# One sequence of heads through both attention mixers of a layer, in a four-layer fp32 transformer kernel

## Chip, cores and metric

The kernel runs on one core of a Trainium2 chip. The metric is the time of one execution on the device in microseconds, the median of several runs. Lower is better.

## What is computed

Two blocks of two layers run one behind the other over a sequence of 512 tokens of width 1024, in fp32. The first block's layers ("A") have three mixers side by side: sliding-window attention with sinks (swa, 6 heads), a pooling mixer, and latent attention with rotary keys (mla, 6 heads). The second block has a recurrent layer ("R") and a layer with forgetting attention (fox, 8 heads, "F"); both also attend to 256 memory tokens (xa, 4 heads). Cut to what matters here:

```
# layer A (twice)
proj  = rms_norm(x, attn_norm) @ w_in
out_a = swa_mixer(...)        # q, k normed per head; band of 128; softmax with a sink
out_b = pool_mixer(...)
out_c = mla_mixer(...)        # keys: a part per head, and one rotated part for all heads
x = x + concat([out_a, out_b, out_c]) @ w_out
x = x + (silu(h @ w_gate) * (h @ w_up)) @ w_down
# layer F (R has the recurrence in the place of fox)
y_mix, xq = fox_group(...)    # causal, decay per key
y_mem = memory_group(xq, mem) # full attention to the memory
x = x + concat([y_mix, y_mem]) @ w_out
x = x + square(relu(h @ w1)) @ w2
```

## The kernel before

Activations lie transposed (features on the partitions, 512 tokens along the row). Every fp32 product with a weight is three passes of TensorE over a high and a low part (`passes`, lines 853, 857 and 858). The weights come in chunks of 1 MB: SyncE loads a chunk into `raw`, GpSimd splits it into `wh` and `wl` (`split`, lines 647 and 652, about 7 us a chunk), TensorE uses it. Each engine has its own program and its own in-order queue, written out by hand; semaphores join them. `Banks` counts the uses of each of the eight PSUM banks.

A mixer is a `Mixer` with its heads, and units of one or two heads. For a unit, `prep` makes the normed queries and keys: TensorE spreads the row scales to banks 6 and 7 (line 1122), VectorE multiplies into `t` (lines 1744, 1752), ScalarE copies the high parts to `qh` and `key` (line 1374), GpSimd subtracts for the low parts (`ql`, `key`, line 697) and gives `qk_ready`, for which VectorE's next `prep` waits. A head then goes like this:

- TensorE, `score_rows` in two halves (banks 0, 1; lines 1158 and 1161 for causal, 1169 and 1171 for the band, 1174 for full): scores by query, for the row maxima;
- VectorE, `maxima` in two halves (lines 2138 to 2152) into `mx`, part of tile `sm`;
- ScalarE, `diagonals` in two halves: the maxima as diagonal blocks `dg`;
- TensorE, `score_columns` (banks 2, 3; lines 1200 to 1209): scores by key, minus the maxima. A causal head has four blocks and uses each of the two banks twice;
- ScalarE, `exponentials` into `pt`; swa adds the sink's exponential, `es`;
- TensorE, `weighted` (bank 4; lines 1226, 1235, 1236, 1241): values times `pt`;
- ScalarE, `reciprocal` (`rt`, logarithm and exponential), VectorE, `out` (`sq`), GpSimd, `mixed`: into `act`. For swa the denominator is first added by VectorE (`es<-ps,es`, in `out`), and `reciprocal` waits for it (`den_ready`); for the others it reads a bank.

The orders within step `hd` of the loop over heads are: TensorE rows of `hd+1` (first half), `prep`, columns of `hd`, rows of `hd+1` (second half), `weighted(hd-1)`; VectorE first maxima of `hd+1`, `prep`, `out(hd-2)`, second maxima; ScalarE `reciprocal(hd-2)`, first diagonals of `hd+1`, `exponentials(hd)`, `prep`, second diagonals; GpSimd `prep`, a weight chunk in two of the heads, `mixed(hd-2)`.

`attention` is called once for each mixer. At the end of the first mixer's loop, in step `hd == m.heads`, `start(nxt)` begins the next: for mla the rotated part of the keys (ts, then a copy and a subtraction into each of the two key tiles) and unit 0. Unit 1 and the first rows follow at the head of the next call:

```
prep(m, 1)
score_rows(0, 0)
score_rows(0, 1)
for hd in range(m.heads + 1):
```

Of the kernel before, what the change touches and what calls it, by code (L numbers as in the profile page):

```python
# [28 lines left out]
P = 128  # L29
# [169 lines left out]
class Mixer:  # L199


    def __init__(self, kind, name, heads, per_unit, rows, scale, tile0, place, kidx):
# [7 lines left out]
    def slot(self, u):  # L210
        return u % 2
# [10 lines left out]
    def half(self, h):  # L222

        return h % 2 if self.per_unit == 2 else 0

# [37 lines left out]
MLA = Mixer("causal", "mla", 6, 1, 96, MLA_SCALE, 5, 1, 6)  # L263
FOX = Mixer("causal", "fox", 8, 2, 64, 1.0, 0, 0, 4)
XA = Mixer("full", "xa", 4, 1, 128, XA_SCALE, 4, 1, 0)


def build(nc, a):
    with ExitStack() as ctx:
# [65 lines left out]
        key_pairs = {"swa": [[key[0], key[1]]], "mla": [[key[0]], [key[1]]], "xa": [[key[0]], [key[1]]],  # L335
# [21 lines left out]
        dgs = {"swa": (dg0, dg1_swa), "mla": (dg0, dg1), "fox": (dg0, dg1), "xa": (dg0, dg1)}  # L357
# [263 lines left out]
        def _(pool):  # L621
# [7 lines left out]
            def split(s, nblk, first=False, slot_done=None, early=False):  # L629
# [4 lines left out]
                if slot_done is not None:  # L634
                    pool.wait_ge(ready[slot_done], bk.filled(slot_done, -1))
# [116 lines left out]
            def summed(hd):  # L752


                if hd >= 2:
                    pool.wait_ge(ready[5], bk.filled(5, hd - 2))
                for b in (2, 3):
                    pool.wait_ge(free[b], bk.emptied(b, hd))
# [3 lines left out]
            def attention(m, nxt=None, chunk_at=None, recurrence=False, second_at=None, slot_done=None):  # L762
                prep(m, 1)
                for hd in range(m.heads + 2):
                    if m.starts(hd):
                        prep(m, m.starts(hd))
                    if m.name == "xa":
                        if hd >= 2:
                            mixed(m.vrow(hd - 2), m.tile(hd - 2))
                        if hd < m.heads:  # L770
                            summed(hd)
                    if hd == chunk_at:

                        split_all(1, BLOCKS)
                    if hd == second_at:

                        split_all(1, BLOCKS, slot_done)
                    if m.name == "mla" and hd == m.heads:
# [3 lines left out]
                    if hd >= 2 and m.name != "xa":  # L782
                        mixed(m.vrow(hd - 2), m.tile(hd - 2))
                    if hd == m.heads and nxt:
                        prep(nxt, 0)
                    if recurrence and hd < 4:
                        mixed(slice(0, P), hd)
                bk.close(m.uses())

            s = 0  # L790
            for l, kind in enumerate(layers):
# [3 lines left out]
                if kind == "A":  # L795
# [3 lines left out]
                    attention(SWA, MLA, 3)  # L799
                    attention(MLA, second_at=3, slot_done=7)  # L800
                elif kind == "R":
                    bk.close(USES_IN_R)
                    prep(XA, 0)
                    attention(XA, None, 2, True, second_at=4, slot_done=3)
# [24 lines left out]
        def _(pe):  # L829
# [295 lines left out]
            def prep(m, u):  # L1125
                spread_to(6, u, u, m.place)
# [3 lines left out]
                elif m.name == "mla":  # L1130
                    spread_to(7, 1 + u, 6 + u // 2, m.place)
                elif m.name == "fox":
                    spread_to(7, u, 4 + u, m.place)
                else:
                    spread_to(7, u, u, 1, M_MEM, slice(64, P))

            def start(m):

                pe.wait_ge(rs_ready, rsr.up(2 if m.name == "xa" else 1))
                if m.name == "mla":  # L1140
                    spread_to(7, 0, 9, m.place)
                prep(m, 0)

            def attention(m, vcols, keys, heads=None, nxt=None, s_pool=None):
# [3 lines left out]
                def score_rows(hd, half):  # L1148
# [1317 lines left out]
```

## Time and profile before

| | |
|---|---|
| median of 3 runs | 2461.61 us (2461.43 to 2462.5) |
| the profiled execution | 2467.87 us, span of its trace 2466.1 us |
| TensorE | busy 2329.9 us (94%), mean granted clock 0.974 |
| GpSimd | busy 1669.3 us (68%) |
| VectorE | busy 1030.9 us (42%) |
| ScalarE | busy 502.2 us (20%) |
| DMA | 84 GB/s over the span |

The profile gives each instruction with its engine, its line and what it waited for. PE is TensorE, DVE is VectorE, ACT is ScalarE and POOL is GpSimd; PEclk is the clock that TensorE was granted, as a share of 2.4 GHz. An idle time in square brackets stands ahead of the instruction on its own engine, with what ended it. Most instructions of the vector engines have the line of a helper, so tiles tell more than lines: `t<-qc` is mla's `prep`, `key<-ts` the rotated part, `es<-ps,es` swa's denominator, `sq<-ps,rt` the product in `out`.

### The profile page before, as it was taken

The page shows a single profiled execution, that of the slowest core. Times are in us where ns is not written, and L with a number is a line of the kernel's source. Part 1 is how long each engine was busy: PE and PEld are TensorE (multiplying, and loading weights), DVE is VectorE, ACT ScalarE, POOL GpSimd, SP SyncE. Part 2 cuts the span into 40 slices and gives each one's busy share as a digit, 9 for nine tenths or more (in the row PEclk, how much of TensorE's full clock was granted, in tenths as well). Part 3 has the DMA queues.
Part 4 walks back from the last instruction along what each step waited for, and adds up shares of the span by engine and source line. Part 5 has one row for each costly group of instructions (what it writes and reads, how often), then busy time and mean ns, then how long its engine had stood idle before and what let it go on. Part 6 is the DMA issues. An engine that isn't in the chain of part 4 may idle for free.

```text
span 2466.1 us, 29684 instructions
## 1 busy us (share of the span) xinstructions
PE 2329.9 (94%) x11024; PEld 1900.3 (77%) x11024; DVE 1030.9 (42%) x1304; ACT 502.2 (20%) x955; POOL 1669.3 (68%) x1378
## 2 busy tenths in 40 slices
PE   6978999999997899999998799999999798999999
PEld 4767788888776678888887478888888676888887
DVE  6663533322366353332237645215334334540430
ACT  3244211110134421111012511001111263100000
POOL 5565677777756567777777677767766566776774
PEclk9988999999998899999999899999999999999999
DMA  4300222223330022222332123222232200222222
GB/s 146 116 18 18 77 94 102 87 85 98 113 108 18 18 79 92 102 92 81 103 116 103 35 85 102 89 98 102 87 118 86 86 35 18 87 101 102 87 101 85
DMA packets 37892, 207.93 MB, mean 84 GB/s; under 512 B 3580, under 2 KB 10364, under 8 KB 16936
## 3 DMA queue, kind: packets, MB, share of 16 engines
q1 hardware_dynamic: 37800, 206.70, 23.9%
q8 instruction: 58, 0.95, 0.2%
q14 instruction: 34, 0.28, 0.0%
HBM read 204.55 MB, written 2.13 MB: 84 GB/s over the span
## 4 chain that ended last, share of the span: by engine, by line
PE 60%; POOL 3%; DVE 2%; ACT 2%; issue 2%; DMA 0%; DVEq 0%; POOLq 0%; ACTq 0%; SPq 0%
PE ps L853 18%; PE ps L857 18%; PE ps L858 18%; POOL wl L652 1%; PE ps L1226 1%; PE ps L1200 1%; ACT rt L1374 1%; PE ps L1241 0%; DMA raw<-w_in_f 0%; POOL wh L647 0%; PE ps L1204 0%; PE ps L1201 0%; PE ps L1202 0%; POOL act L737 0%; DVE sq L1744 0%
## 5 line engine op out<-in xcount | busy, mean ns | idle before, releaser
L652 POOL TENSOR_TENSOR wl<-raw,wh 128x512 fp32r<-128x512 f32 (+1 forms) x776 | 1030.5, 1360 | 0.2
L647 POOL TENSOR_SCALAR wh<-raw 128x1024 fp32r<-128x1024 f32 (+1 forms) x388 | 427.8, 1122 | 586.9 <-PE ps L853 458.5
L853 PE MATMUL ps<-h,wh 128*128 128x512 f32 x1576 | 619.2, 393 | 27.1 <-DVE h L1752 20.2
L858 PE MATMUL ps<-h,wl 128*128 128x512 f32 x1576 | 615.2, 390 | 0.0
L857 PE MATMUL ps<-h,wh 128*128 128x512 f32 x1576 | 615.0, 390 | 0.0
L853 PE MATMUL ps<-act,wh 128*128 128x512 f32 x1120 | 437.4, 391 | 1.0 <-DVE x L1744 1.0
L857 PE MATMUL ps<-act,wh 128*128 128x512 f32 x1120 | 436.0, 389 | 0.0
L858 PE MATMUL ps<-act,wl 128*128 128x512 f32 x1120 | 435.9, 389 | 0.0
L853 PEld LDWEIGHTS ps<-h,wh 128*128 128x128 f32 x1576 | 296.8, 188 | 95.9 <-issue 24.7
L857 PEld LDWEIGHTS ps<-h,wh 128*128 128x128 f32 x1576 | 297.1, 189 | 61.8 <-issue 1.0
L858 PEld LDWEIGHTS ps<-h,wl 128*128 128x128 f32 x1576 | 296.8, 188 | 62.0
L1744 DVE TENSOR_TENSOR x<-x,ps 128x512 f32<-128x512 f32 x80 | 55.0, 688 | 482.7 <-PE ps L858 482.1
L853 PEld LDWEIGHTS ps<-act,wh 128*128 128x128 f32 x1120 | 210.5, 188 | 46.9 <-issue 3.1
L857 PEld LDWEIGHTS ps<-act,wh 128*128 128x128 f32 x1120 | 210.4, 188 | 44.0 <-issue 0.5
L858 PEld LDWEIGHTS ps<-act,wl 128*128 128x128 f32 x1120 | 210.4, 188 | 43.7
L1374 ACT ACTIVATE h<-x,vec 128x512 fp32r<-128x512 f32 x64 | 46.3, 724 | 438.3 <-DVE x L1744 430.9
L1374 ACT ACTIVATE act<-t 128x512 f32 (+1 forms) x64 | 40.5, 633 | 461.4 <-DVE t L1752 461.4
L697 POOL TENSOR_TENSOR ql<-t,qh 128x512 fp32r<-128x512 f32 x30 | 38.9, 1296 | 132.5 <-ACT key L1374 94.3
L1744 DVE TENSOR_TENSOR t<-ps,rstd 128x512 f32<-128x512 f32 x108 | 74.7, 692 | 107.7 <-PE ps L858 106.4
L1744 DVE TENSOR_TENSOR ssq<-ssq,sq 128x512 f32<-128x512 f32 (+1 forms) x80 | 80.7, 1008 | 85.6 <-ACT sq L1374 84.8
L1744 DVE TENSOR_TENSOR nt<-ps,rstd 128x512 f32<-128x512 f32 x44 | 30.4, 692 | 194.1 <-PE ps L858 194.0
L1744 DVE TENSOR_TENSOR act<-t,act 128x512 f32 (+1 forms) x64 | 67.7, 1058 | 64.1 <-ACT act L1374 64.1
(324 smaller groups left out, 2672.2 us busy)
## 6 DMA issues: line engine op xcount, KB each, us to landing
raw<-w_gu SPq DMA_DIRECT2D x44, 1024.0 KB, 4.8
raw<-w_up SPq DMA_DIRECT2D x32, 1024.0 KB, 4.8
raw<-w_down_b SPq DMA_DIRECT2D x32, 1024.0 KB, 4.8
raw<-w_down_a SPq DMA_DIRECT2D x32, 704.0 KB, 4.0
raw<-w_in_a SPq DMA_DIRECT2D x14, 1024.0 KB, 4.9
raw<-w_in_f SPq DMA_DIRECT2D x13, 1024.0 KB, 4.9
raw<-w_in_r SPq DMA_DIRECT2D x11, 1024.0 KB, 4.9
raw<-w_out_a SPq DMA_DIRECT2D x8, 1024.0 KB, 8.1
```

Of the source, the lines that this page charges most:

```text
L647: pool.tensor_scalar(hi_s[:, part], raw[s][:, part], 1.0, 1.0, ALU.mult, ALU.mult).then_inc(hi_done, 1)
L652: return pool.tensor_tensor(lo_s[:, part], raw[s][:, part], hi_s[:, part].bitcast(F32), ALU.subtract)
L697: pool.tensor_tensor(out, in0, in1, op).then_inc(hi_done, 1)
L853: first = pe.matmul(out, w_hi, v_hi, start=start, stop=False)
L857: pe.matmul(out, w_hi, v_lo, start=False, stop=False)
L858: return pe.matmul(out, w_lo, v_hi, start=False, stop=stop)
L1200: pe.matmul(out, k_hi[:, kc], qh[s][:, qc_], start=True, stop=False)
L1226: last = pe.matmul(ps[4][:, j * P:T], vcols(hd, j), pt[:, j * T:j * T + n], start=j == 0, stop=j == keys - 1)
L1374: return sc.activation(out, in_, f, **kw)
L1744: dve.tensor_tensor(out, in0, in1, op).then_inc(sig.sem, 1)
```

## The change

`attention` takes a sequence of mixers, (swa, mla) or (fox, xa), and runs one loop over all their heads, numbered `g`. Its last two steps belong to the sequence and no longer to each mixer. `begins` says at which step a unit is prepared: units 0 and 1 of the later mixer in the last two steps of the earlier one. The first rows of the later mixer are scored in the step ahead of its first head, as for any head. The rotated part of mla's keys has its own function, `rotation`, in step `g == 3`. For these overlaps mla gets key tiles of its own, `key_mla`, a second `dg` tile of its own, and the other of the two query slots; `use` adds the earlier mixer's uses of a bank to the count. GpSimd's chunks stand at steps 3 and 9 for (swa, mla), and at 4 and 7 for (fox, xa); in each loop a `prep` stands ahead of the chunk. The layer with xa alone makes one call as before. The diff, cut to its core:

```diff
+        self.earlier = after.uses() if after else {}
+    def use(self, b, u):
+        return self.earlier.get(b, 0) + u
     def slot(self, u):
-        return u % 2
+        return (u + (self.name == "mla")) % 2
...
+XA_F = Mixer("full", "xa", 4, 1, 128, XA_SCALE, 4, 1, 0, FOX)
+ROTATE_AT = 3
+def begins(seq):
+    at, first = {}, 0
+    for i, m in enumerate(seq):
+        if i:
+            at[first - 2], at[first - 1] = (m, 0), (m, 1)
+        for hd in range(m.heads):
+            if m.starts(hd):
+                at[first + hd] = (m, m.starts(hd))
+        first += m.heads
+    return at
...
+        key_mla = [view(f"key_mla{s}", A_AT + 32768 + 29696 + s * 4096, [2, T], F32R) for s in range(2)]
+        dg1_mla = view("dg1_mla", A_AT + 32768 + 45056, [TB, P], F32R)
...
# GpSimd
+            def attention(seq, chunks_at, recurrence=False):
+                prep(seq[0], 1)
+                for g in range(n + 2):
+                    if g in at:
+                        prep(*at[g])
+                    cross = g < n and order[g][0].name == "xa"
+                    if cross:
+                        if g >= 2:
+                            finished(g)
+                        summed(*order[g])
+                    if g in chunks_at:
+                        split_all(1, BLOCKS, chunks_at[g])
...
+                    if g >= 2 and not cross:
+                        finished(g)
...
-                    attention(SWA, MLA, 3)
-                    attention(MLA, second_at=3, slot_done=7)
+                    attention((SWA, MLA), {3: None, 9: (7, 2)})
...
-                    attention(FOX, XA, 4, second_at=7, slot_done=0)
-                    attention(XA)
+                    attention((FOX, XA_F), {4: None, 7: (0, -1)})
...
# TensorE
+                prep(seq[0], 1)
+                score_rows(*order[0], 0)
+                score_rows(*order[0], 1)
+                for g in range(n + 1):
+                    if g + 1 < n:
+                        score_rows(*order[g + 1], 0)
+                    if g in at:
+                        m, u = at[g]
+                        if u == 0 and m.name == "xa":
+                            start(m)
+                        else:
+                            prep(m, u)
+                    if seq[-1].name == "mla" and g == ROTATE_AT:
+                        rotation()
+                    if g < n:
+                        score_columns(*order[g])
...
+                    if g + 1 < n:
+                        score_rows(*order[g + 1], 1)
+                    if g:
+                        weighted(*order[g - 1])
...
# ScalarE
+                for g in range(n + 2):
+                    if g >= 2:
+                        reciprocal(*order[g - 2])
+                    if g + 1 < n:
+                        diagonals(*order[g + 1], 0)
+                    if g < n:
+                        exponentials(*order[g])
+                    if g in at:
+                        prep(*at[g], order[g])
+                    if g + 1 < n:
+                        diagonals(*order[g + 1], 1)
...
# VectorE
+            def rotation():
+                b, u = 7, MLA.use(7, 0)
+                dve.wait_ge(ready[b], bk.filled(b, u))
+                r = slice(64, P)
+                tt(ts[r, :], krp[r, :], ps[b][r, :], ALU.mult, bk.empties(b, u))
+                for both in key_mla:
+                    split(ts[r, :], both[r, 0, :], both[r, 1, :], chain)
...
+                for g in range(n + 2):
+                    if g + 1 < n:
+                        maxima(*order[g + 1], 0)
+                    if g in at:
+                        m, u = at[g]
+                        prep(m, l, u)
+                    if seq[-1].name == "mla" and g == ROTATE_AT:
+                        rotation()
...
+                    if g >= 2:
+                        out(*order[g - 2])
+                    if g + 1 < n:
+                        maxima(*order[g + 1], 1)
```

## Rows read from the trace of the kernel before

**Rows 1.** The page's part 4: the chain by line, shares of the span.

```profile
PE ps L853 18%; PE ps L857 18%; PE ps L858 18%; POOL wl L652 1%; PE ps L1226 1%; PE ps L1200 1%; ACT rt L1374 1%; PE ps L1241 0%; DMA raw<-w_in_f 0%; POOL wh L647 0%; PE ps L1204 0%; PE ps L1201 0%; PE ps L1202 0%; POOL act L737 0%; DVE sq L1744 0%
```

**Rows 2.** Windows, layer 2: us, busy of PE, PEld, DVE, ACT, POOL; PEclk, DMA, GB/s.

```profile
765.00:788.00 23.00, 20.87 (x166) 19.56 (x165) 12.22 (x21) 15.37 (x32) 14.57 (x14) 1.00 0.14 47
788.00:806.00 18.00, 11.42 (x34) 7.93 (x35) 11.92 (x19) 6.91 (x14) 9.07 (x8) 0.58 0.00 0
806.00:846.00 40.00, 37.57 (x194) 30.44 (x192) 16.68 (x30) 25.39 (x58) 21.55 (x19) 0.94 0.04 11
```

**Rows 3.** Timeline, TensorE, layer 2, swa to mla: start, us, engine, line; idle before.

```profile
791.62 0.79 PE L1122 MATMUL ps<-rs,spread 64*128 64x512 f32 x1 [3.07 <-DVE ts L1744]
...
803.29 0.47 PE L1158 MATMUL ps<-key,qh 128*128 128x128 f32 x1 [1.65 <-ACT key L1374]
...
805.48 0.79 PE L1200 MATMUL ps<-qh,key 128*128 128x512 f32 x1
```

**Rows 4.** Timeline, layer 2, head 4 of swa: TensorE, VectorE, ScalarE.

```profile
776.03 0.38 PE L1200 MATMUL ps<-qh,key 128*128 128x256 f32 x1 [0.18 <-ACT dg L1374]
...
777.23 0.69 DVE L1744 TENSOR_TENSOR es<-ps,es 64x512 f32<-64x512 f32 x1
...
777.96 0.63 ACT L1374 ACTIVATE rt<-es 64x512 f32<-64x512 f32 x1 [1.98 <-DVE es L1744]
...
779.34 0.68 DVE L1744 TENSOR_TENSOR sq<-ps,rt 64x512 f32<-64x512 f32 x1 [1.42 <-issue]
...
782.26 0.69 ACT L1374 ACTIVATE dg_swa<-ident,sm 128x128 fp32r<-128x128 f32 x2 [0.86 <-DVE sm L2152]
...
783.01 0.39 PE L1200 MATMUL ps<-qh,key 128*128 128x256 f32 x1 [1.10 <-ACT dg_swa L1374]
```

**Rows 5.** Timeline, TensorE, layer 2: first column product of mla's heads 1 and 2.

```profile
813.95 0.50 PE L1200 MATMUL ps<-qh,key 128*128 128x512 f32 x1
...
821.19 0.50 PE L1200 MATMUL ps<-qh,key 128*128 128x512 f32 x1
```

**Rows 6.** VectorE in head 3; copy and subtraction of key and of cqn; GpSimd's split.

```profile
770.28 0.24 DVE L2152 TENSOR_SCALAR sm<-sm,vec 128x2 f32<-128x2 f32 x1
...
773.87 0.69 DVE L2147 TENSOR_REDUCE sm<-ps 128x2 f32<-128x512 f32 x1 [0.67 <-PE ps L1171]
...
L1748 DVE TENSOR_SCALAR key<-ts x4: 424/424/425, 174.6 to 793.7; 64x512 fp32r<-64x512 f32 x4
L1744 DVE TENSOR_TENSOR key<-ts,key x4: 689/1164/1643, 175.1 to 794.2; 64x512 fp32r<-64x512 f32 x4
...
L1748 DVE TENSOR_SCALAR cqn<-t x4: 1398/1402/1411, 69.4 to 692.9; 128x512 fp32r<-128x512 f32 x4
L1744 DVE TENSOR_TENSOR cqn<-t,cqn x4: 693/1179/1667, 70.8 to 694.4; 128x512 fp32r<-128x512 f32 x4
...
771.47 5.00 POOL L652 TENSOR_TENSOR wl<-raw,wh 128x512 fp32r<-128x512 f32 x4
```

**Rows 7.** Timeline, VectorE, mla's head 1: the next unit waits for GpSimd.

```profile
815.51 0.69 DVE L1744 TENSOR_TENSOR t<-qc,ps 128x512 f32<-128x512 f32 x1 [1.69 <-POOLq L750]
```

**Rows 8.** Windows, layer 2: behind two idle stretches; the granted clock is PEclk.

```profile
744.80:750.00 5.20, 5.19 (x25) 5.20 (x26) 3.42 (x12) 1.18 (x3) 4.68 (x6) 0.52 0.00 0
...
852.40:856.00 3.60, 3.60 (x7) 1.91 (x8) 0.00 (x0) 0.00 (x0) 3.06 (x3) 0.56 0.02 5
```

**Rows 9.** Timeline, last layer, fox to xa: GpSimd's split and first sum; TensorE.

```profile
2024.70 5.00 POOL L652 TENSOR_TENSOR wl<-raw,wh 128x512 fp32r<-128x512 f32 x4
...
2033.19 2.42 PE L1226 MATMUL ps<-pt_f,vof 128*128 128x512 f32 x8 [1.70 <-DVE sq L1744]
...
2040.94 0.80 PE L1174 MATMUL ps<-key,qh 128*128 128x256 f32 x2 [4.21 <-ACT key L1374]
...
2050.04 1.28 POOL L760 TENSOR_TENSOR ts<-pt 128x512 f32<-128x512 f32 x1 [0.24 <-POOL key L697]
...
2065.55 1.98 PE L1241 MATMUL ps<-pt0b,fxv 128*128 128x512 f32 x4 [2.14 <-DVE sq L1744]
```

More of the change, by code:

```diff
@@ L750, in prep, with summed @@
                 pool.sem_inc(qk_ready, 1)
-            def summed(hd):
+            def summed(m, hd):
                 if hd >= 2:
-                    pool.wait_ge(ready[5], bk.filled(5, hd - 2))
+                    pool.wait_ge(ready[5], bk.filled(5, m.use(5, hd - 2)))
                 for b in (2, 3):
-                    pool.wait_ge(free[b], bk.emptied(b, hd))
+                    pool.wait_ge(free[b], bk.emptied(b, m.use(b, hd)))
                 pt = pts["xa"][hd % 2]
                 pool.tensor_tensor(pt_sum[hd % 2], pt[:, 0:T], pt[:, T:2 * T], ALU.add).then_inc(sum_ready, 1)
[L762 to L778, printed above, removed]
@@ new lines, in attention, with finished @@
+            def attention(seq, chunks_at, recurrence=False):
+                order, at = heads_of(seq), begins(seq)
+                n = len(order)
+                def finished(g):
+                    m, hd = order[g - 2]
+                    mixed(m.vrow(hd), m.tile(hd))
+                prep(seq[0], 1)
[9 more added lines that the diff above has]
+                        split_all(1, BLOCKS, chunks_at[g])
+                    if g == n and seq[-1].name == "mla":
@@ L790, in _ @@
+                    if recurrence and g < 4:
+                        mixed(slice(0, P), g)
+                for m in seq:
+                    bk.close(m.uses())
             s = 0
@@ L1238, in weighted @@
                     else:
-                        for j in range(keys):
-                            pe.wait_ge(free[2 + j], bk.emptied(2 + j, hd))
+                        for j in range(m.key_blocks()):
+                            pe.wait_ge(free[2 + j], bk.emptied(2 + j, m.use(2 + j, hd)))
                             last = pe.matmul(ps[4][:, :], vcols(hd, j), pt[:, j * T:(j + 1) * T],
@@ L2121, in start, with rotation, attention, maxima @@
                     halves(key_pairs[m.name][0])
-                if m.name == "mla":
-                    dve.wait_ge(ready[7], bk.filled(7, 0))
-                    r = slice(64, P)
-                    tt(ts[r, :], krp[r, :], ps[7][r, :], ALU.mult, bk.empties(7, 0))
-                    for s in range(2):
-                        split(ts[r, :], key[s][r, 0, :], key[s][r, 1, :], chain)
-                prep(m, l, 0)
-            def attention(m, l, nxt=None):
-                def maxima(hd, half):
+                prep(m, l, 0)
+            def rotation():
+                b, u = 7, MLA.use(7, 0)
[4 more added lines that the diff above has]
+                    split(ts[r, :], both[r, 0, :], both[r, 1, :], chain)
+            def attention(seq, l):
+                def maxima(m, hd, half):
                     mxs = mx[hd % 2]
```

240 lines of the change are left out of this document (101 added, 139 removed).

## The prediction

> **What bounds the kernel now.** I read the page first: TensorE is busy 94% of the span, and the chain that ended last runs through TensorE, more than half the span in the three lines of the weight products, which the change leaves alone [rows 1]. So a gain or a loss can only come from stretches in which TensorE waits. Next I cut the three attention stages with a change of mixer into windows. In the second layer TensorE works 20.9 of 23 us while the six heads of swa run at full clock, 11.4 of 18 us across the change to mla at a granted clock of 0.58, and 37.6 of 40 us among the heads of mla [rows 2]. The first layer has the second's idle times to 0.01 us, plus one more of 1.36. Then the timeline gave the waits behind the hole: 3.07 us ended by VectorE (the rotated key part) and 1.65 us ended by ScalarE (key), with two smaller ones between them 6.6 in all [rows 3], 7.9 in the first layer. In the last layer, from fox to xa, it is 1.70 and 4.21 us [rows 9]. These are what the change can take away; the reader should see that they are a drained pipeline, and that it drains for 22.5 us between the score columns of swa's last head (783.01) and those of mla's first (805.48) [rows 3, 4].
>
> **Costs of nothing.** `use()`, `heads_of` and `begins` are worked out as the program is built. The new views `key_mla` and `dg1_mla` and mla's other slot issue nothing. The layer with one mixer keeps its order. SyncE's queue isn't touched. What is left is order, so I follow the start of each head's score columns, numbered c0, c1 and so on through the joined sequence, in the second layer. Before: c4 at 776.03, c5 783.01, c6 (mla's first head) 805.48, c7 813.95, c8 821.19 [rows 3 to 5]. From c8 on the order is the old one.
>
> **How I check the arithmetic.** In head 4 as it is, `out(2)` starts es at c4+1.20, ScalarE's logarithm follows at +1.93, VectorE's product at +3.31 to +3.99, the diagonal at +6.23, and c5 comes at +6.98 [rows 4]. One point matters for all that follows: VectorE runs `out` ahead of `maxima(.., 1)`, ScalarE runs `reciprocal` ahead of `diagonals(.., 0)` and `exponentials`, and both queues are in order. For swa the reciprocal waits for es of VectorE. So what is put ahead of `out` in VectorE's queue delays the reciprocal, the exponentials and the next diagonals.
>
> **Step 1, the rotation in head 3.** It takes 0.69 us for ts, and twice a copy and a subtraction. In the hole these took 0.42 and 0.69 to 1.64, but in head 3 GpSimd splits a weight chunk until 776.5 [rows 6]. The nearest rows of the same pair beside a split are cqn's, 1.40 and a median of 1.18 [rows 6]. Lower bound 0.69+2(0.42+0.69)+0.2 = 3.1, upper 0.69+2(1.40+1.67) = 6.8 with the longest cqn subtraction; I take the cqn medians, since the split runs throughout, 0.69+2(1.40+1.18)+0.15 = 6.0. VectorE comes free at 770.52 [rows 6], so es starts at 776.55, the product ends 2.8 us later at 779.3, the diagonal starts 2.24 us behind that (both distances from [rows 4]) and takes 0.7, so c4 = 782.3, **+6.3** (lower bound +3.3). TensorE idles 773.8 to 779.4, since `weighted(2)` waits for bank 4. The stall of 3.07 us is moved, not hidden: all that covers it in head 3 is the 0.67 us for which VectorE waits ahead of the maxima [rows 6]. Trainium skill, "SBUF — State Buffer", section "Who interferes with whom": an SBUF to SBUF tensor_scalar in a two-port mode and a GpSimd instruction exclude each other. It would give the 1.40; by the clean 0.42 and 0.69 the head would be 2.9 us shorter. By that rule the cqn row, with its 1.40 beside a split, agrees.
>
> **Step 2, head 4 takes mla's first unit.** VectorE does 0.69+0.74 us ahead of es, ScalarE 1.15 between exponentials and the last diagonals. es at +2.05, product to +4.85, reciprocals to +4.1, exponentials and es to +6.4, copies (`qh`, `key`) to +7.55, diagonal to +8.25. TensorE has the first rows of mla and two spreads more, 1.1 us, and waits for `key`: c5 = c4+8.8 = 791.1; before 6.98, so **+1.8**.
>
> **Step 3, head 5, second unit.** VectorE's `prep` waits for GpSimd's ql and key remainder: 1.27+1.27 us after `key`, as VectorE's t waits for GpSimd today [rows 7]; so, from c5, t starts at +1.6, es +3.1, product to +5.9, exponentials and es to +7.45, copies to +8.6. c6 = c5+9.8 = 800.9. Before 22.47: **-12.7**. Here is the whole gain.
>
> **Step 4, heads 6 and 7 (mla 0 and 1).** Here a new wait appears. Causal columns use banks 2 and 3 twice, so block 2 waits for the exponential of block 0. That stands in ScalarE's queue behind the reciprocal of swa's head 4, behind VectorE's es, behind `prep`, behind GpSimd. Counted from c6: GpSimd 1.5, prep 3.05, es 3.8, reciprocal 5.15, diagonal 5.85, exponential 6.45; TensorE stood since 2.1, **4.4 us idle**. Then columns to 7.6, rows 8.35, `weighted` 10.1 (1.8 us that used to run in the hole), rows and spreads: c7 = c6+11.25 = 812.15 (before 8.47, +2.8). Head 7 likewise, with es at +2.05, block 2 at 5.45 (3.3 us idle) and mla's own `weighted` 2.4: c8 = c7+10.85 = 823.0 (before 7.24, +3.6). From head 8 on the reciprocals are mla's, which wait for TensorE alone.
>
> Sum at the clock as it is: +6.3+1.8-12.7+2.8+3.6 = **+1.8 us** a layer; with the clean rotation -1.2.
>
> **Step 5, the clock.** Behind the idle 741.3 to 744.8, the stretch 744.8 to 750.0 ran at 0.52, which is the lower of the two levels, 1.2 GHz; behind 848.7 to 852.4, 3.6 us at 0.56 [rows 8]. That costs 5.2 x 0.48 = 2.5 and 3.6 x 0.44 = 1.6 us of TensorE's work. Before has such a stretch after its own hole, and it is in its c values. After has three idles of over 3 us (5.6, 4.4, 3.3), each ahead of work that is on the chain: 3 x 2.2 = **+6.5 us** a layer. Bounds: 0, and about 15 if the clock stays down from 778 to 822, as it did for 20 us from 791 on.
>
> **Step 6, fox to xa.** c6 and c7 of fox slip by 0.4 and 1.4 (two spreads and xa's rows), xa's first columns come at 2033.6 instead of 2042.38. But in head 7 GpSimd now does xa's `prep` 1 first, which waits for ScalarE until 2031.8, and only then the split of 7.1 us that ended at 2029.7 [rows 9]. So `prep` (2.0 us) to 2033.9, split to 2041.1, `mixed` (1.9) to 2043.0, `prep` 2 to 2045.1, `mixed` to 2047.0, the first sum (1.28) to 2048.3; before it ended at 2051.3 [rows 9]. VectorE's prep of unit 3 waits for 2045.1 with `out(7)` behind it, so xa's first `weighted` comes at 2047.1, TensorE idle for 5.6 us. The tail then runs in today's rhythm of one head per 5 us, its last `weighted` at 2061.8 instead of 2065.55 [rows 9]: **-3.8 us**, of 8.8.
>
> **Total.** 2 x (1.8+6.5) - 3.8 = +12.8 us. The profiled execution took 2467.87 us (span 2466.1), so 2480.7 by its clock; the median of the three runs is 6.3 lower, 2461.61, so **2474**.
>
> **Rivals.** (a) *The clock falls no more than before* (for: the second layer holds 1.00 from 765 to 788 through idles of 1.1 us; against: all six idles over 3 us in these stages are followed by the lower level): 2 x 1.8-3.8 = 0, **2462**. With the clean rotation 2456. (b) *The clock stays down over the joint*: 2 x (1.8+15)-3.8, **2491**. (c) *The join works as it reads*, faster: rotation, prep and reciprocals lie in VectorE's and ScalarE's spare time (VectorE is busy 12.2 of 23 us), and the holes go, 6.6+7.9+5.9 = 20.4, with some of the low clock: **2440**. It holds if block 2 of mla's columns doesn't wait; against it stands the order of the two queues. (d) *It isn't overlapped at all*, mla's first rows waiting for swa's end: against it, `key` of mla's first unit is due at 789.9, before c5; then the hole stays and head 4's 1.8 us is added: **2465**.
>
> **Chances.** Forecast 0.43, (a) 0.24, (b) 0.10, (c) 0.19, (d) 0.04. A measurement of this kernel tells 0.2%, 4.9 us, from no change. (a) is split over no change and faster, (c) is faster: faster 0.25, same 0.22, slower 0.53. The range leaves out most of (c) and the edge of (b): 2451 to 2491; the forecast's own range is 2467 to 2484.
>
> **What would show it.** Right: a wait of about 5 us of TensorE in head 3 that ends with a diagonal or bank 4, es of `out(1)` some 6 us behind the maxima, copies of the rotation near 1.4; in mla's first two heads the third block of columns waiting on pt for 4.4 and 3.3 us; a granted clock of about 0.5 behind each; in the last layer the GpSimd split at about 2034 and `weighted` of xa waiting for it; swa's last to mla's first columns near 10 us. Wrong: if c4 comes less than 4 us later, if c4 to c8 takes clearly less than 41 us, or the clock reads 1.00 across them.

## The result: 0.8% slower

The changed kernel takes 2485.09 us (median of 4 runs, 2480.67 to 2486.93), the kernel before beside it 2462.06 (2461.43 to 2464.39): a ratio of 1.0076, 95% interval 1.0063 to 1.009. The forecast was 2474, slower, in a range of 2451 to 2491. The profiled execution took 2486.93 us, its span is 2485.2 against 2466.1.

The page of the kernel after, its parts 1 (busy time of each engine) and 4 (the chain that ended last, by line), beside the table of before and [rows 1]:

```profile
PE 2338.3 (94%) x11024; PEld 1908.4 (77%) x11024; DVE 1030.7 (41%) x1304; ACT 499.7 (20%) x955; POOL 1670.7 (67%) x1378
...
PE ps L886 18%; PE ps L890 18%; PE ps L891 18%; POOL wl L684 2%; PE ps L1264 1%; POOL wh L679 1%; PE ps L1236 1%; POOL act L769 1%; DMA raw<-w_in_f 0%; ACT rt L1416 0%; PE ps L1279 0%; DVE t L1795 0%; PE ps L1240 0%; PE ps L1237 0%; PE ps L1238 0%
```

The busy times of VectorE, ScalarE and GpSimd move by under 3 us. GpSimd's split (`wh`, `wl`) has come into the chain with 3%, where it had 1%. So the question is again where TensorE stands. For that I laid the same VectorE instruction at the end of each stage of the two traces side by side and took the differences of the two starts. These are worked out from the rows, not rows themselves:

| stage | after later than before, at its end | added in it | forecast |
|---|---|---|---|
| first layer (swa, mla), with the stage behind it | +3.5 us | +3.5 | +8.3 |
| second layer, likewise | +10.8 | +7.3 | +8.3 |
| third layer (xa alone, with the recurrence) | +18.0 | +7.2 | 0 |
| last layer (fox, xa) | +19.1 | +1.1 | -3.8 |

Each line is one execution of each kernel, and it scatters. The kernels of experiments 1 and 8 have the same code in the first two layers as the kernel after, and add 3.3 and 5.6 us, and 6.2 and 5.9 us there. The kernel of experiment 2 has the code of before in them, and adds -2.4 and -0.1 us. So a line of the table is good to 2 or 3 us.

**Layer 2.** Timeline of TensorE after the change: the first column product of head 3 (c3) and so on to c8, and the waits between them; answers to [rows 3 to 5]. mla's heads begin with c6; the line of c6 or c7 is followed by that of their block 2, the third of their four blocks of columns.

```profile
773.63 0.39 PE L1236 MATMUL ps<-qh,key 128*128 128x256 f32 x1
...
783.03 0.80 PE L1274 MATMUL ps<-pt,vos 128*128 128x128 f32 x2 [5.60 <-DVE sq L1787]
...
787.36 0.39 PE L1236 MATMUL ps<-qh,key 128*128 128x256 f32 x1
...
796.05 0.38 PE L1236 MATMUL ps<-qh,key 128*128 128x256 f32 x1
...
802.21 0.49 PE L1274 MATMUL ps<-pt,vos 128*128 128x128 f32 x2 [2.26 <-DVE sq L1787]
...
806.93 0.79 PE L1236 MATMUL ps<-qh,key_mla 128*128 128x512 f32 x1
...
812.40 0.38 PE L1236 MATMUL ps<-qh,key_mla 128*128 128x256 f32 x1 [2.02 <-ACT pt L1416]
...
818.61 0.50 PE L1236 MATMUL ps<-qh,key_mla 128*128 128x512 f32 x1
...
823.51 0.48 PE L1236 MATMUL ps<-qh,key_mla 128*128 128x256 f32 x1 [2.83 <-ACT pt_a L1416]
...
831.98 0.50 PE L1236 MATMUL ps<-qh,key_mla 128*128 128x512 f32 x1
```

The join does what it says: from the last head of swa to the first of mla (c5 to c6) there are 10.9 us where there were 22.5. What it takes comes back around it: c3 to c4 takes 13.7 us (before 6.0, c3 stood at 770.03), c6 to c7 11.7 (8.5), c7 to c8 13.4 (7.2). c3 to c8 is 58.35 us against 51.16.

What head 3 waits for stands in VectorE's queue. Timeline of VectorE after, head 3; and GpSimd's split of the same time. Answers to [rows 6].

```profile
773.89 0.23 DVE L2199 TENSOR_SCALAR sm<-sm,vec 128x2 f32<-128x2 f32 x1
774.15 0.69 DVE L1787 TENSOR_TENSOR ts<-krp,ps 64x512 f32<-64x512 f32 x1
774.88 0.51 DVE L1791 TENSOR_SCALAR key_mla<-ts 64x512 fp32r<-64x512 f32 x1
775.42 1.65 DVE L1787 TENSOR_TENSOR key_mla<-ts,key_mla 64x512 fp32r<-64x512 f32 x1
777.11 1.38 DVE L1791 TENSOR_SCALAR key_mla<-ts 64x512 fp32r<-64x512 f32 x1
778.53 1.63 DVE L1787 TENSOR_TENSOR key_mla<-ts,key_mla 64x512 fp32r<-64x512 f32 x1
780.20 0.68 DVE L1787 TENSOR_TENSOR es<-ps,es 64x512 f32<-64x512 f32 x1
...
775.08 6.21 POOL L684 TENSOR_TENSOR wl<-raw,wh 128x512 fp32r<-128x512 f32 x4
```

Between the maxima and `es` of `out(1)` lie 6.05 us of rotation, and behind `es` the reciprocal, the product and `weighted(2)`, as in [rows 4].

The clock, windows after in layer 2 (us, busy of PE, PEld, DVE, ACT, POOL; PEclk, DMA, GB/s); answers to [rows 2, 8]:

```profile
779.20:786.00 6.80, 2.96 (x14) 2.97 (x15) 3.26 (x5) 4.07 (x9) 4.02 (x4) 0.51 0.44 154
...
803.10:809.90 6.80, 6.80 (x23) 5.35 (x22) 3.13 (x6) 2.17 (x5) 4.44 (x4) 0.50 0.00 0
...
823.60:830.40 6.80, 6.80 (x20) 4.97 (x21) 1.25 (x2) 2.63 (x7) 2.83 (x3) 0.50 0.01 2
```

With one of 3.4 us from 813.3 on (PEclk 0.52) these are four spells at the lower level (1.2 GHz), 23.8 us in sum. The first begins within the idle time of 5.60 us, the others start behind those of 2.26, 2.02 and 2.83; before there is one of 20.5 us (790.6 to 811.1, PEclk 0.50).

**Third layer.** This was not foreseen. Timeline of GpSimd, first before, then after: the split of the second chunk (`wh`, `wl`) and the first operation of the mixes of cross heads 2 and 3 (`act<-sq`).

```profile
1424.98 0.62 POOL L701 TENSOR_SCALAR act<-sq 128x512 fp32r<-128x512 f32 x1
...
1427.17 2.07 POOL L647 TENSOR_SCALAR wh<-raw 128x1024 fp32r<-128x1024 f32 x2 [0.22 <-POOL act L737]
1429.20 5.02 POOL L652 TENSOR_TENSOR wl<-raw,wh 128x512 fp32r<-128x512 f32 x4
1434.31 0.62 POOL L701 TENSOR_SCALAR act<-sq 128x512 fp32r<-128x512 f32 x1
```

```profile
1438.14 2.06 POOL L679 TENSOR_SCALAR wh<-raw 128x1024 fp32r<-128x1024 f32 x2 [0.22 <-POOL act L769]
1440.16 5.02 POOL L684 TENSOR_TENSOR wl<-raw,wh 128x512 fp32r<-128x512 f32 x4
1445.27 0.62 POOL L733 TENSOR_SCALAR act<-sq 128x512 fp32r<-128x512 f32 x1
```

`cross = g < n and ...` is false at g = 4, where the second chunk stands. So `finished(4)`, the mix of cross head 2, moved from ahead of the split to behind it, and now two mixes wait behind 7.1 us of splitting: the one at 1445.27 and, from 1447.32 on, that of head 3. TensorE's output projection waits for the first of them, 1.90 us until 1447.29, and runs at a granted clock of 0.83 for the 10.1 us behind it.

### The profile page after: what moved, and what is told of

Same layout as the page of the kernel before. It is cut to its first block, busy times and chain, and to the rows that moved or that the text cites. A ratio compares the mean times of both kernels' runs of the same rounds, so it can differ in the third digit from the quotient of the medians.

```text
span 2485.2 us, 29688 instructions
## 1 busy us (share of the span) xinstructions
PE 2338.3 (94%) x11024; PEld 1908.4 (77%) x11024; DVE 1030.7 (41%) x1304; ACT 499.7 (20%) x955; POOL 1670.7 (67%) x1378
## 3 DMA queue, kind: packets, MB, share of 16 engines
q1 hardware_dynamic: 37800, 206.70, 23.8%
## 4 chain that ended last, share of the span: by engine, by line
PE 59%; POOL 4%; DVE 2%; issue 2%; ACT 2%; DMA 0%; DVEq 0%; POOLq 0%; ACTq 0%; SPq 0%
PE ps L886 18%; PE ps L890 18%; PE ps L891 18%; POOL wl L684 2%; PE ps L1264 1%; POOL wh L679 1%; PE ps L1236 1%; POOL act L769 1%; DMA raw<-w_in_f 0%; ACT rt L1416 0%; PE ps L1279 0%; DVE t L1795 0%; PE ps L1240 0%; PE ps L1237 0%; PE ps L1238 0%
## 5 line engine op out<-in xcount | busy, mean ns | idle before, releaser
L886 PE MATMUL ps<-h,wh 128*128 128x512 f32 x1576 | 619.9, 393 | 26.0 <-DVE h L1795 19.1
```

Source lines behind the costliest of these rows:

```text
L886: first = pe.matmul(out, w_hi, v_hi, start=start, stop=False)
```

## The experiments

Times are medians; a ratio is to the kernel before on the same chip, with its 95% interval. Its median lay between 2462.06 and 2468.01 us from one set of runs to another, so kernels are compared by their ratios. "Stage" is the difference to before at the end of each stage, as in the table above, from the one profiled execution.

**1. The one-mixer layer's order as before.** In GpSimd's `attention`, in the kernel after:

```diff
-                    cross = g < n and order[g][0].name == "xa"
+                    cross = order[min(g, n - 1)][0].name == "xa"
                     if cross:
                         if g >= 2:
                             finished(g)
-                        summed(*order[g])
+                        if g < n:
+                            summed(*order[g])
```

> The changed kernel with one edit: in the layer with xa alone GpSimd does mixed of head 2 ahead of the weight chunk again, as before the change. Theory (the order of GpSimd's queue in that layer costs, 5.0 us from the last mixed to the first x): TensorE's out projection no longer waits 1.9 us for mixed of head 2, the layer gives back about 5 us, 2480 us. Rival (what that layer lost is only the phase of the clock): no change, 2485.

2478.75 us, ratio 1.005 (1.0033 to 1.0067). By the ratios that is 6.4 us less than after. The stage of the third layer adds -0.05 us instead of +7.2.

**2. The same order put into the kernel before, alone.** There the mix of cross head 2 goes behind the chunk; that of head 3 stood behind it already (1434.31 in the rows before):

```diff
+                    late = recurrence and hd >= m.heads
                     if m.name == "xa":
-                        if hd >= 2:
+                        if hd >= 2 and not late:
                             mixed(m.vrow(hd - 2), m.tile(hd - 2))
...
-                    if hd >= 2 and m.name != "xa":
+                    if hd >= 2 and (m.name != "xa" or late):
```

> The kernel before, with one part of the change alone: in the layer with one mixer (four cross heads) GpSimd splits the second chunk of weights ahead of mixed(2) and mixed(3), as the kernel after does. Theory: that order costs by itself what this layer lost, the queue of 5.0 us of subtractions in front of the last two mixes, so the layer's stage grows by 4 to 5 us and the time by the same, near 2467 (ratio 1.0018). Rival: the layer was longer only because its columns fell into other clock periods; then this kernel is at 2462, ratio 1.000, and the last mix follows the split with nobody waiting for it.

2472.99 us, ratio 1.0028 (1.0015 to 1.004), which is 6.9 us (3.7 to 9.9). The stage of that layer adds 5.0 us. Timeline of TensorE, the first product of the output projection that waits for the mix, and the window behind it (granted clock 0.79):

```profile
1431.87 0.50 PE L854 MATMUL ps<-act,wh 128*128 128x512 f32 x1 [3.31 <-POOL act L737]
```

```profile
1431.87:1440.00 8.13, 8.13 (x29) 6.51 (x30) 0.00 (x0) 0.00 (x0) 1.91 (x2) 0.79 0.26 109
```

So one moved mix costs about 5 us by itself: 3.3 us of waiting, and 1.7 behind it, where the products run at the lower clock. In the kernel after, 3.8 of the 7.2 us come at the place of the mix and 3.3 ahead of it, where the granted clock was 0.91 against 0.94 before. The kernel of experiment 12, whose order in this layer is repaired, has 3.2 us there too, also at 0.91. So I read these 3.3 us as scatter of the clock from execution to execution, but no run isolates them. In kernels that kept the moved order the stage added 4.0 to 7.2 us.

**3. The rotation in two pieces**, behind the second maxima of steps 3 and 4:

```diff
-                    if seq[-1].name == "mla" and g == ROTATE_AT:
-                        rotation()
...
                     if g + 1 < n:
                         maxima(*order[g + 1], 1)
+                    if seq[-1].name == "mla" and g in (ROTATE_AT, ROTATE_AT + 1):
+                        rotation(g - ROTATE_AT)
```

(`rotation(0)` makes ts and the first split, `rotation(1)` the second split.)

> The changed kernel with the rotation in two pieces, each behind the second maxima: ts and the first key tile at the end of step 3, the second key tile at the end of step 4. Theory (the rotation ahead of out(1) holds the den, the reciprocal and bank 4): columns 3 to 4 fall from 13.7 us to about 6.5, columns 4 to 5 rise by 1 to 1.5, the first piece is partly beside the split; 5 to 6 us a layer, 2474 us. Rival (head 3 is held by something else, the split or the exponentials): c3 to c4 stays over 11 us, 2485.

2475.57 us, ratio 1.0037 (1.0025 to 1.005). Timeline of VectorE, the five instructions of the rotation, then TensorE's c3, c4, c5 with a wait between:

```profile
773.79 0.69 DVE L1787 TENSOR_TENSOR ts<-krp,ps 64x512 f32<-64x512 f32 x1
774.52 0.74 DVE L1791 TENSOR_SCALAR key_mla<-ts 64x512 fp32r<-64x512 f32 x1
775.29 0.99 DVE L1787 TENSOR_TENSOR key_mla<-ts,key_mla 64x512 fp32r<-64x512 f32 x1
...
782.96 0.42 DVE L1791 TENSOR_SCALAR key_mla<-ts 64x512 fp32r<-64x512 f32 x1
783.42 0.69 DVE L1787 TENSOR_TENSOR key_mla<-ts,key_mla 64x512 fp32r<-64x512 f32 x1
```

```profile
768.53 0.38 PE L1236 MATMUL ps<-qh,key 128*128 128x256 f32 x1
...
774.97 0.38 PE L1236 MATMUL ps<-qh,key 128*128 128x256 f32 x1
...
781.88 0.80 PE L1274 MATMUL ps<-pt_a,vos 128*128 128x128 f32 x2 [3.13 <-DVE sq L1787]
...
787.07 0.58 PE L1236 MATMUL ps<-qh,key 128*128 128x256 f32 x1
...
802.06 0.58 PE L1236 MATMUL ps<-qh,key_mla 128*128 128x256 f32 x1 [4.38 <-ACT pt L1416]
```

c3 to c4 is back at 6.4 us, c4 to c5 went from 8.7 to 12.1. The five instructions take 3.5 us in sum, not the 5.9 of the kernel after: GpSimd's split ends at 774.98, within the first copy, and GpSimd is idle beside the second piece. c3 to c8 is 52.7 us, 5.6 less than after.

**4. The whole rotation, uncut, behind the second maxima of step 3**, which tells place from cut:

```diff
-                    if seq[-1].name == "mla" and g == ROTATE_AT:
-                        rotation()
...
                     if g + 1 < n:
                         maxima(*order[g + 1], 1)
+                    if seq[-1].name == "mla" and g == ROTATE_AT:
+                        rotation()
```

> The kernel after, with the whole rotation still in step 3 but behind the second maxima instead of ahead of swa's output. It tells the rotation's place from its being cut in two. With two pieces behind the second maxima, c3 to c4 was 6.44 us and c4 to c5 12.1 (18.5 together, after: 22.4), and VectorE's five instructions took 0.69, 0.74, 0.99, 0.42 and 0.69 us, 3.5 together, where in the kernel after, beside GpSimd's split of weights, they took 6.0. Theory: place does it: the rotation stands behind GpSimd's split, is short, and holds up no output of step 3; c3 to c5 is again 18 to 19 and the time near the run with two pieces, 2476. Rival: the cut does it: the second split, now in a row with the first, holds up the maxima of step 4 and the two outputs behind them, c3 to c5 is 20 to 22 us, and the time 2480 or more.

2479.55 us, ratio 1.005 (1.0034 to 1.0067). c3 to c4 6.4 us, c4 to c5 14.1, together 20.6: both theories have a part. In the profiles the place gives 1.9 us (22.4 to 20.6) and the cut another 2.0 (to 18.5); in the first layer it is 2.8 and 1.4 (22.7, 20.0, 18.5). The intervals of the two times overlap, so the time alone doesn't tell the cut from the uncut rotation. The rotation's own instructions take 4.5 us here, 5.9 after and 3.5 in two pieces. The cut keeps the second split from the front of step 4, where it holds up two maxima, mla's `prep` and `out(2)` behind them.

**5. Products that nobody reads in the idle times** of the kernel after (20 in head 3, 12 and 10 ahead of block 2 in mla's first two heads):

```diff
+                    if seq[-1].name == "mla" and g == 3:
+                        pe.wait_ge(free[7], bk.emptied(7, MLA.use(7, 0)))
+                        for _ in range(20):
+                            pe.matmul(ps[7][:, :], neg_ones_r[:, :], qh[SWA.slot(1)][:, :], start=True, stop=True)
                     if g:
                         weighted(*order[g - 1])
...
+                        if m.name == "mla" and j == 2 and hd < 2:
+                            pe.wait_ge(free[5], bk.emptied(5, SWA_HEADS - 1))
+                            for _ in range((12, 10)[hd]):
+                                pe.matmul(ps[5][:, :], neg_ones_r[:, :], qh[s][:, :], start=True, stop=True)
```

> The changed kernel with products that nobody reads in TensorE's three long idle times of a layer: 20 of 128x512 ahead of weighted(2) in step 3, 12 and 10 ahead of block 2 of the columns of mla's heads 0 and 1. Nothing is waited for less. Theory (part of the loss is TensorE at the lower clock behind its idle times, 5.4 us of the 58.3 from columns 3 to 8): the clock reads 1.00 there and a layer gains about 4 us, 2477 us. Rival (the chain is all latency of the other engines, the clock costs nothing): the same time or up to 3 us more, 2485 to 2488.

2478.69 us, ratio 1.0044 (1.0027 to 1.006). Window of layer 2, from c3 to the idle time of head 7:

```profile
771.99:820.00 48.01, 39.03 (x243) 33.01 (x243) 26.08 (x42) 21.26 (x48) 21.18 (x19) 1.00 0.06 23
```

The granted clock is 1.00 up to 820; one spell at the lower level follows (0.62 in 821.6 to 825). The five distances from c3 to c8 are 12.61, 8.70, 9.93, 11.05 and 13.24 us, 55.5 in sum, against 58.35 after, and 56.6 and 56.9 in the kernels of experiments 1 and 8 with the same code. By the ratios the time is 7.9 us less, 3.9 a layer.

**6. The same in the kernel before**: 13, 6 and 7 unread products in the three idle times of TensorE in the change of mixer.

```diff
                 elif m.name == "mla":
+                    if u == 0:
+                        pe.wait_ge(free[5], bk.emptied(5, SWA.heads - 1))
+                        unread(13)
                     spread_to(7, 1 + u, 6 + u // 2, m.place)
...
+                        if m.name == "mla" and (hd, i) == (0, 2):
+                            unread(6)
...
+                    if m.name == "mla" and hd == 1 and half == 0:
+                        unread(7)
```

> The kernel before, with 13, 6 and 7 products of 512 columns, whose result nobody reads, in the three idle times of TensorE between the mixers (3.07, 1.41 and 1.65 us in layer 2). Nothing in the order or the waits of the other work is changed. It prices the clock by itself: before, the granted clock is at its lower level from 790.6 to 811.1, and the first mla columns stand in it. Theory: that low clock follows from the idle times and costs 4 to 7 us a layer (the busy time of 793 to 811, about 13 us, at half speed, less what waits for other engines anyway), so 2450 to 2456, ratio 0.996, and the stretch from c5 to c6 falls from 22.5 to about 19. Rival: the clock falls from what was done before the idle times or the columns are held up by other engines, and nothing is gained: 2462 or, with the products in the way, 2464.

2463.25 us, ratio 0.9982 (0.9972 to 0.9992): a real gain, but small. Windows of the same stretch of layer 2, before and with the products:

```profile
790.60:811.10 20.50, 15.97 (x52) 12.54 (x52) 12.16 (x20) 7.12 (x15) 9.07 (x8) 0.50 0.00 1
```

```profile
790.00:811.00 21.00, 17.45 (x88) 13.88 (x87) 13.01 (x23) 11.37 (x26) 9.56 (x8) 0.92 0.01 2
```

The clock is mostly held up, and the gain is smaller than the 4 to 7 us a layer of the theory: the ratio gives 4.4 us for both layers, 2.2 each. The profiles say 3.1 and 3.4, but before's profiled execution was 6 us above its median, and the unchanged first layer of experiment 2 is already 2.4 us shorter than its own. In layer 2, c5 to c6 falls by only 0.9 us and c6 to c7 by 2.4; in layer 1, c5 to c6 doesn't fall at all (22.77 against 22.47). So of the 22.5 us hole at most one microsecond is TensorE's clock.

**7. VectorE's outputs of swa ahead of mla's preparation** (steps 4 to 7):

```diff
                     if g + 1 < n:
                         maxima(*order[g + 1], 0)
+                    first = g >= 4 and order[g - 2][0].name == "swa"
+                    if first:
+                        out(*order[g - 2])
                     if g in at:
                         m, u = at[g]
                         prep(m, l, u)
...
-                    if g >= 2:
+                    if g >= 2 and not first:
                         out(*order[g - 2])
```

> The changed kernel with VectorE doing out of swa's heads 2 to 5 ahead of prep of mla's units instead of behind it (steps 4 to 7). Theory (es behind prep holds the reciprocal, and with it the exponentials and block 2): columns 4 to 8 fall from 44.6 us to about 33, the idle ahead of block 2 from 2.0 and 2.8 us to under 1.7; 11 us a layer, 2463 us. Rival (block 2 waits for its own columns and exponential, not for the queue): 4 to 8 stays over 42 us, 2485.

2458.44 us, ratio 0.9971 (0.996 to 0.9981): faster than before, with the rotation still in head 3 and the third layer's moved mix still in. Timeline of TensorE, c3, c4, c6 and c8 with two waits (c5 and c7 stand at 783.14 and 797.59):

```profile
761.43 0.39 PE L1236 MATMUL ps<-qh,key 128*128 128x256 f32 x1
...
770.83 0.80 PE L1274 MATMUL ps<-pt,vos 128*128 128x128 f32 x2 [5.61 <-DVE sq L1787]
...
775.78 0.38 PE L1236 MATMUL ps<-qh,key 128*128 128x256 f32 x1
...
789.95 0.50 PE L1236 MATMUL ps<-qh,key_mla 128*128 128x512 f32 x1
...
792.99 0.38 PE L1236 MATMUL ps<-qh,key_mla 128*128 128x256 f32 x1 [0.98 <-ACT pt L1416]
...
805.91 0.50 PE L1236 MATMUL ps<-qh,key_mla 128*128 128x512 f32 x1
```

The rotation's wait stays (5.61). From c4 on the distances are 7.4, 6.8, 7.6 and 8.3 us, 30.1 in sum, where the kernel after has 44.6 and before has 45.2. The waits for block 2 fall to 0.98 and 1.07 us, those ahead of `weighted` in heads 4 and 5 are gone, and from 777 to c8 the granted clock is 1.00. The 14.5 us that c4 to c8 is shorter are the delays of steps 2 to 4 and the spells of low clock that came with them; the time is 5 us below what was expected.

**8. The outputs of fox ahead of xa's preparation**, likewise (`g >= 6` in the last layer alone).

> The kernel after, with the last two outputs of fox (steps 8 and 9, and those of steps 6 and 7) ahead of the cross mixer's preparation on VectorE. In the kernel after, TensorE idles 5.83 us before the cross mixer's first weighted sums (2060.94 to 2066.77) until VectorE's output of fox head 7, which stands behind a preparation that waited 5.53 us for GpSimd. Theory: VectorE's place in line is what is waited for, the idle time falls to about 1 us, and 3 to 5 us of it reach the end, 2481 (ratio to before 1.006). Rival: GpSimd's split (2053.1 to 2060.2) is the bound through the cross mixer's own units, and the idle time comes back one head later: no change, 2485.

2484.51 us, ratio 1.0075 (1.0063 to 1.0087): no change that can be measured. The idle time of 5.83 us has become one of 3.25 and, behind the first `weighted`, one of 1.47 until GpSimd's sum for xa. Timeline of TensorE at the last join, and of VectorE's output of fox head 7:

```profile
2062.88 3.43 PE L1279 MATMUL ps<-pt,fxv 128*128 128x512 f32 x4 [3.25 <-DVE sq L1787]
```

```profile
2062.13 0.69 DVE L1787 TENSOR_TENSOR sq<-ps,rt 64x512 f32<-64x512 f32 x1 [4.48 <-POOL act L769]
```

The output now waits for GpSimd's mix, which is queued behind the split. So GpSimd's split holds this join, wherever VectorE's output stands.

**9. Four repairs together**: experiments 1, 3, 7 and 8 in one kernel.

> The kernel after with four repairs together: GpSimd's order in the one-mixer layer as before, the rotation's two splits in two steps (3 and 4) behind the second maxima, VectorE's outputs of swa ahead of mla's preparation (steps 4 to 7), and those of fox ahead of the cross mixer's. If the repairs add up, from the run with the outputs ahead (2458.4): -4.9 for the one-mixer layer, -5 in each attention layer for the rotation (there 14.35 us from c3 to c4, 6.44 with the rotation in two, less what its second piece costs in the next step), -3 at the last join: 2441, ratio 0.991. Rival: the second piece pushes the preparation of mla's second unit in step 5, whose lateness was hidden so far, and half of the rotation's gain goes: 2447.

2443.01 us, ratio 0.991 (0.9895 to 0.9924). Window of layer 2 from c3 to c8, before, after, and here:

```profile
770.03:821.19 51.16, 42.28 (x230) 35.29 (x230) 27.47 (x46) 26.77 (x57) 26.07 (x24) 0.80 0.06 21
```

```profile
773.63:831.98 58.35, 43.81 (x230) 37.01 (x230) 28.07 (x47) 25.51 (x57) 27.25 (x24) 0.80 0.05 19
```

```profile
758.04:798.68 40.64, 34.44 (x229) 29.36 (x229) 27.66 (x46) 25.79 (x57) 23.04 (x21) 1.00 0.08 27
```

The same 229 or 230 products; 40.6 us instead of 51.2 or 58.4, at a granted clock of 1.00 throughout. VectorE does 27.5 to 28.1 us of work in each of the three: what changed is its order.

**10. The same, with the rotation's pieces in steps 2 and 3** (`ROTATE_AT = 2`).

> As the run with all four repairs, but the rotation's two pieces in steps 2 and 3, ahead of any of mla's preparations. Theory: in step 3 a piece behind the second maxima moved nothing (c3 to c4 6.44 us), in step 4 one did (c4 to c5 12.1 us); a piece in step 2 meets swa's last preparation (unit 2) and costs under 2 us, so this is 2 to 4 us a layer better than with steps 3 and 4: 2436. Rival: step 2 is as full as step 4 and nothing is gained, 2441 to 2445.

2448.58 us, ratio 0.9932 (0.9921 to 0.9944). No better, by the medians rather worse: c3 to c8 is 42.7 us, with 2.3 us of idle ahead of `weighted` in head 3 and a granted clock of 0.88. Nothing is gained, as the rival had it, though its time was 2441 to 2445.

**11. and 12. GpSimd's second chunk of the last layer in step 6 or 5 instead of 7**, on top of the four repairs (`{4: None, 6: (0, -1)}`, `{4: None, 5: (0, -1)}`).

> The kernel with all four repairs, and GpSimd's split of the second chunk in the last layer one step earlier (step 6, behind the cross mixer's first preparation, instead of step 7). With only VectorE's outputs moved ahead the idle time at the last join stayed at 3.25 and 1.47 us, the first until fox head 7's output, which waited 4.48 us for GpSimd's mix, queued behind the split (2052.9 to 2060.0). Theory: GpSimd's split in step 7 is the bound; in step 6 it fills 3.1 us in which GpSimd was idle, and 2 to 4 us go: 2440, ratio 0.990. Rival: it only moves the wait to the cross mixer's second preparation, within 1 us of the kernel with four repairs (2443).

> The same with the split in step 5, where GpSimd was idle 3.7 us before the cross mixer's first preparation. Theory: it ends near 2045, 2 us after that preparation could have begun, and hides more than in step 6: 2 to 5 us less than with four repairs, 2439. Rival: with the first chunk's split just one step earlier (2028 to 2035), outputs of fox wait for the mixes behind it, and as much comes back: 2443.

2441.51 us, ratio 0.9883 (0.9867 to 0.9899), and 2441.98, ratio 0.9886 (0.9871 to 0.99). Timeline of TensorE at the last join with the chunk in step 5: fox's last `weighted`, xa's first, and the largest wait left.

```profile
2017.71 2.39 PE L1265 MATMUL ps<-pt_f,vof 128*128 128x512 f32 x8
...
2023.23 1.88 PE L1280 MATMUL ps<-pt,fxv 128*128 128x512 f32 x4
...
2039.79 1.98 PE L1280 MATMUL ps<-pt0b,fxv 128*128 128x512 f32 x4 [2.14 <-DVE sq L1788]
```

The stage of the last layer adds -0.4 us with the four repairs, -3.0 with the chunk in step 6 and -9.7 in step 5, the 5.83 us idle time gone. The times don't show this difference: the two medians lie within 0.5 us, and both intervals overlap that of experiment 9. In the profile of the step 5 kernel 3.2 us come back in the third layer, ahead of the changed place, where the granted clock was 0.91 against 0.94 before. These are the fastest kernels of the study, 1.1 to 1.2% under before.

## Why the prediction was right, and where not

The sign and the main mechanism held. By the profiled executions +12.8 us was forecast and +19.1 came (by the medians, +12 and +23). The 6.3 between are a layer that was set to nothing (+7.2), the last layer (+4.9), and the two first layers, which lost less than forecast (-4.8 and -1.0). That the total came so near is in part luck: misses of +12.1 and -5.8 partly cancel. By the medians the loss is nearly twice the forecast; 2485 lies in the stated range and 1 us outside the forecast's own of 2467 to 2484.

**Step 1 (rotation in head 3)** held: c4 is +7.7 us later (forecast +6.3), +6.6 at full clock (experiment 5). The rotation took 6.05 us where 6.0 was taken, but from other parts: the copies 0.51 and 1.38 for 1.40 twice, the subtractions 1.65 and 1.63 for 1.18 twice. Experiments 3 and 4 gain by moving and cutting the rotation, but its duration falls with it (5.9, 4.5 and 3.5 us), so no run prices the slowness alone. The section that the prediction cites (the Trainium skill, "SBUF — State Buffer", "Who interferes with whom") says more than the tensor_scalar rule: an instruction of VectorE with two inputs in SBUF, as each of these subtractions is, contends with one of GpSimd that reads SBUF. The trace agrees with both: the copy takes 0.42 clear of GpSimd and 1.38 beside it, the subtraction 0.69 and up to 1.65.

**Steps 2 to 4** held once the clock is taken out, but for the last distance: forecast distances c4 to c8 were 8.8, 9.8, 11.25 and 10.85; experiment 5 has 8.70, 9.93, 11.05, and 13.24 for the last, which holds a spell of low clock and a block 2 that comes 6.3 us behind c7 (4.9 after). The waits for block 2 were forecast at 4.4 and 3.3 us and came as 2.02 and 2.83. The first was shorter because the columns ahead of it ran at half speed: with full clock there (experiment 3) it is 4.38. The second is 2.75 in experiment 3, so it was forecast half a microsecond too long. Not named was the wait of 2.26 us ahead of `weighted` in head 5; it is inside step 3's distance.

**Step 5 (clock)**: forecast +6.5 a layer, beyond steps 1 to 4. In layer 2, c3 to c8 took 58.35 us against 52.97 by the steps, so +5.4; the same code took 56.6 and 56.9 in experiments 1 and 8, so +3.7 and +3.9 there. Filling the idle times gave back 3.9 us a layer by the ratios. So the term was right in kind and too large by 1 to 3 us. Its condition was not what happened: it counted three idle times of over 3 us, and they came as 5.60, 2.26, 2.02 and 2.83, with a spell at the lower level at each. In layer 1 c3 to c8 grew only from 52.67 to 56.92, +4.3 for a forecast of +8.3. That is mostly the execution of before that it is held against: it had longer distances at low clock in that layer (8.09 and 8.70 for c6 to c8), while the same code in experiment 2 took 49.55, and by that layer 1 grew by 7.4. How much of the miss is the forecast's own these runs don't tell.

**Step 6 (last layer)**: forecast -3.8, came +1.1, of which about 1.4 us lie ahead of the attention. The mechanism is right: TensorE idles 5.83 us (5.6 forecast) until the work behind GpSimd's split, as experiments 8, 11 and 12 show. What failed is the sentence that the tail then runs in today's rhythm. From xa's first `weighted` to its last it took 17.9 us (2066.77 to 2084.63), before 14.8. Behind the idle time the window reads:

```profile
2066.80:2072.80 6.00, 6.00 (x9) 2.90 (x10) 0.77 (x2) 1.20 (x3) 5.56 (x6) 0.50 0.01 3
```

Step 6 had an idle time of over 3 us and no clock term behind it, against its own step 5.

**"The layer with one mixer keeps its order"** is the step that failed outright: a term of 0 that measured +7.2 us, 5.0 of them shown by experiment 2, where the moved mix stands alone; the rest I read as scatter. The sentence was read off the call, which is unchanged, and not off the loop that the call runs through, whose condition now ends two steps earlier.

**The rivals.** (c), that the join works as it reads, was worth 2440, and the repaired kernel takes 2443, 0.9% under before: the gain was there, and the order of VectorE's queue, with one mix in GpSimd's, kept it away. The sum agrees better than its terms: (c) has 5.9 us from the last join, where the repaired kernel has 0.4, and 14.5 us and some clock from the first two, where it has 21.2. (c) was put at 0.19 "if block 2 of mla's columns doesn't wait", and experiment 7 brought that wait down to about 1 us. (d), not overlapped, is out: c5 to c6 is 10.9 us. (a) is out too, as the clock does fall behind the new waits; (b) would have needed 15 us a layer.

## What to carry to other kernels

When work is pulled forward into a pipeline that is running, look up what stands behind it in each in-order queue: put it behind the step's outputs that others wait for, and cut it so that each piece fits a gap. A loop that is rewritten for one of its callers changes order for all of them; write out each engine's queue for the callers that "aren't touched". And an idle time of some microseconds is to be priced together with the slow columns behind it.

## What the runs showed of the hardware

The granted clock read 1.00 over the 40.6 us of experiment 9, whose longest idle time is 1.3 us, and about 0.5 at or behind each of the idle times of 2.0 to 5.6 us in layer 2 of the kernel after. What such a spell costs isn't read off its length: the 20.5 us at 0.50 in the second layer of the kernel before were worth 2 to 3.5 us, since other engines paced that stretch, and 6 us of it behind the idle time of the last layer cost 3.0. Nor does the length of an idle time alone say that a spell follows: that of 2.25 us ahead of `weighted` in head 5 of experiment 5 (until 799.45) was followed by 1.00, that of 2.26 at the same place in the kernel after by 0.50.

VectorE's copy and subtraction of 64x512 took 0.42 and 0.69 us with GpSimd idle, and up to 1.38 and 1.65 beside GpSimd's split. GpSimd pays as well: its four subtractions took 6.21 us beside the rotation and 5.00 in the same head before. So the same rotation took 5.9 us at one place in the queue and 3.5 in two pieces at another; how much of that 2.3 reached the end no run isolates.
